# Past keys of the paged cache loaded two rows to a partition in a hybrid decoder step on Trainium2

## The reference

```python
k_past = cache_k_diff[l][page_table].reshape(db, PAST_LEN, N_HEADS_DIFF, 2, HEAD_DIM)
v_past = cache_v_diff[l][page_table].reshape(db, PAST_LEN, N_HEADS_DIFF, DIFF_V_DIM)
...
s_past = jnp.einsum('bqhcd,bkhcd->bchqk', q, k_past, preferred_element_type=jnp.float32) * SCALE
...
p = jax.nn.softmax(jnp.concatenate([s_past, s_new], axis=-1), axis=-1)
w = p[:, 0] - lam * p[:, 1]
o = (jnp.einsum('bhqk,bkhe->bqhe', w[..., :p_len], v_past.astype(jnp.float32))
     + jnp.einsum('bhqk,bkhe->bqhe', w[..., p_len:], v_new.astype(jnp.float32)))
```

## Time and profile before

| | |
|---|---|
| median of 3 runs | 1122.25 us (1115.1, 1124.65, 1122.25) |
| the profiled execution | 1113.92 us, its span 1112.1 us |
| TensorE matmul / VectorE / ScalarE / GpSimd busy | 969.6 / 668.9 / 505.7 / 133.9 us |
| DMA packets | 174933, 310.98 MB, 280 GB/s in the mean |
| key pages from the cache | 256 transfers of 256 KB, the last issued at 439.7 us |
| value pages from the cache | 256 transfers of 256 KB |

### The profile page before, as it was taken

How to read it: one execution, slowest core, us unless ns; L and a number is a source line. 1 busy time by engine, 2 the same in 40 slices (tenths; PEclk the granted TensorE clock), 3 DMA queues, 4 the chain that set the end, 5 groups by cost and what they waited for, 6 DMA issues and landing times.

```text
span 1112.1 us, 29337 instructions
## 1 busy us (share of the span) xinstructions
PE 969.6 (87%) x11050; PEld 858.7 (77%) x11050; DVE 668.9 (60%) x1627; ACT 505.7 (45%) x1116; POOL 133.9 (12%) x69
## 2 busy tenths in 40 slices
PE   3989898998887779887889667899999999999995
PEld 3978787777764557676667554699999999999994
DVE  5389645675458887754346445788888888700003
ACT  5654543374125656645234262455555555611123
POOL 1322111111000010002111000000000000133330
PEclk8999999999988999888899787899999999999997
DMA  8699999999999999888979798386768686974632
GB/s 249 248 314 346 320 328 344 358 340 334 317 340 338 337 365 329 301 273 293 327 245 298 221 255 223 123 302 264 301 263 301 263 301 252 325 248 159 228 128 85
DMA packets 174933, 310.98 MB, mean 280 GB/s; under 512 B 13601, under 2 KB 87714, under 8 KB 173282
## 3 DMA queue, kind: packets, MB, share of 16 engines
q1 hardware_dynamic: 172898, 305.24, 80.3%
q10 hardware_dynamic: 1920, 4.20, 1.4%
HBM read 302.30 MB, written 73.92 MB: 338 GB/s over the span
## 4 chain that ended last, share of the span: by engine, by line
PE 32%; issue 30%; DMA 11%; SPq 11%; DVE 7%; ACT 7%; ACTq 0%; POOL 0%; DVEq 0%; POOLq 0%
PE ps L1383 11%; DMA v_ring<-in_cache_v_diff 6%; SPq L666 5%; PE ps L1038 5%; PE ps L1270 4%; PE ps L1232 4%; SPq L768 4%; DVE kt_sb L2153 2%; ACT q_st L1678 2%; PE ps L1189 2%; DMA k_ring<-in_state_v_win 2%; DMA k_ring<-in_cache_k_diff 2%; PE ps L1115 1%; DMA v_ring<-in_state_v_win 1%; ACT s_sb L1723 1%
## 5 line engine op out<-in xcount | busy, mean ns | idle before, releaser
L2153 DVE STREAM_TRANSPOSE kt_sb<-k_ring 128x512 f32<-128x512 f32 x336 | 220.5, 691 | 86.5 <-DMA k_ring<-in_cache_k_diff 37.4
L1270 PE MATMUL ps<-v_ring,pt_sb 128*32 128x128 f32 (+1 forms) x2496 | 98.8, 306 | 62.1 <-DMA v_ring<-in_cache_v_diff 49.3
L1270 PEld LDWEIGHTS ps<-v_ring,pt_sb 128*32 128x32 f32 (+1 forms) x2496 | 75.7, 121 | 78.1 <-issue 67.8
L1038 PE MATMUL ps<-h_hi,w_hi 128*128 128x288 f32 x384 | 124.4, 324 | 1.9 <-DVE h_lo L2006 1.9
L1038 PE MATMUL ps<-h_lo,w_hi 128*128 128x288 f32 x384 | 115.0, 299 | 0.0
L1038 PE MATMUL ps<-h_hi,w_lo 128*128 128x288 f32 x384 | 114.7, 299 | 0.0
L1232 PE MATMUL ps<-kt_sb,q_st 128*32 128x128 f32 (+1 forms) x2816 | 97.0, 281 | 10.2 <-DVE q_st L2163 4.6
L989 POOL TENSOR_TENSOR c_lo<-c_raw,c_hi 128x1408 fp32r<-128x1408 f32 x14 | 46.6, 3332 | 440.2 <-ACT c_hi L1781 440.2
L1232 PEld LDWEIGHTS ps<-kt_sb,q_st 128*32 128x32 f32 x2816 | 72.9, 114 | 28.2 <-issue 19.9
L1038 PEld LDWEIGHTS ps<-h_hi,w_hi 128*128 128x128 f32 x384 | 74.0, 193 | 16.1 <-issue 13.8
L949 POOL TENSOR_TENSOR w_lo<-w_raw,w_hi 128x1024 fp32r<-128x1024 f32 x24 | 57.3, 2390 | 229.5 <-ACT w_hi L1492 229.5
(11 more groups left out here) (236 smaller groups left out, 2289.4 us busy)
## 6 DMA issues: line engine op xcount, KB each, us to landing
k_ring<-in_cache_k_diff SPq DMA_DIRECT2D x256, 256.0 KB, 5.5
v_ring<-in_cache_v_diff SPq DMA_DIRECT2D x256, 256.0 KB, 5.5
out_k_win_sample<-in_state_k_win SPq DMA_DIRECT2D x32, 1020.0 KB, 8.3
out_v_win_sample<-in_state_v_win SPq DMA_DIRECT2D x32, 1020.0 KB, 8.5
k_ring<-in_state_k_win SPq DMA_DIRECT2D x32, 512.0 KB, 7.7
w_raw<-in_w_in SPq DMA_DIRECT2D x24, 512.0 KB, 6.3
g_raw<-in_w_gate SPq DMA_DIRECT2D x11, 1024.0 KB, 5.2
g_raw<-in_w_up SPq DMA_DIRECT2D x11, 1024.0 KB, 5.2
```

The costliest lines, as they stand in the source:

```text
L1038: last = nc.tensor.matmul(M[c][:, 0:HALF], wt, act[:, k, c * HALF:(c + 1) * HALF], start=k == 0 and at_first, stop=k == KT - 1 and act is ...
L1270: last = nc.tensor.matmul(O[32 * f:32 * f + 32, P * h:P * h + P], pt_sb[0:rows, 4 * f + b, :], values[:, f * P:(f + 1) * P], start=g == 0 ...
L2153: V.transpose(kt_sb[:, i, :], k_ring[:, i, :]).then_inc(kt_done, 1)
```

## The change

The past keys of the cache (`it < 4`) go two rows to a partition: page `i` goes to the 64 even partitions if `i` is even and to the 64 odd ones if it is odd, and its rows `2 u` and `2 u + 1` go to the two slots `i - i % 2` and the next. A slot of `k_ring` then holds every second row of two pages, half each, so a transpose waits for both pages of its pair, and a load waits until both slots of its pair have been turned. The transposes of slots 1 and 2 of a half exchange their places in `kt_sb`. The matmuls of the scores write their 4 x 32 columns with steps, as (slot, u, c) into (u, slot, c), c being two neighbouring columns; the result stands in `S` in the order that the values have, and `keep_scores` reads it straight instead of by steps of 32. The windowed items stay as they were.

```diff
                         src = state_pair(sk, q, i)
-                    at_first = i - (it >= 4 and n == 4)
-                    sp.dma_start(k_ring[:, at_first:i + 1, :].squeeze(1) if at_first == i else k_ring[:, at_first:i + 1, :], src)\
-                        .then_inc(k_landed[i], 16)
+                    if it < 4:
+                        dst, src = k_ring[i % 2:P:2, i - i % 2:i - i % 2 + 2, :], src.rearrange("(u r) c -> u r c", r=2)
+                    else:
+                        dst = k_ring[:, i - 1:i + 1, :] if n == 4 else k_ring[:, i, :]
+                    sp.dma_start(dst, src).then_inc(k_landed[i], 16)
...
-                        sp.wait_ge(kt_done, PAGE_NO[last, i] + 1 if i % 4 < pages_of(last) else half_end(last, h))
+                        sp.wait_ge(kt_done, PAGE_NO[last, i | 1] + 1 if i % 4 < pages_of(last) else half_end(last, h))
...
-                        last = nc.tensor.matmul(S[32 * f:32 * f + 32, c0:c0 + 32 * n], q_st[:, h, f, r, :],
+                        scores = S[32 * f:32 * f + 32, c0:c0 + 32 * n]
+                        if it < 4:
+                            scores = scores.rearrange("p (u x c) -> p x u c", x=4, c=2)
+                        last = nc.tensor.matmul(scores, q_st[:, h, f, r, :],
                                                 kt_sb[:, 4 * h:4 * h + n, c:c + 32], start=r % 2 == 0, stop=r % 2 == 1)
...
-                at_load = key_load(t, i)
-                dve.wait_ge(k_landed[at_load], K_LANDS[t, at_load])
+                for page in (i - i % 2, i | 1) if t < FIRST[4] else (key_load(t, i),):
+                    dve.wait_ge(k_landed[page], K_LANDS[t, page])
                 if t:
                     dve.wait_ge(scored if i >= 4 else half_scored, t)
-                V.transpose(kt_sb[:, i, :], k_ring[:, i, :]).then_inc(kt_done, 1)
+                to = i - i % 4 + (0, 2, 1, 3)[i % 4] if t < FIRST[4] else i
+                V.transpose(kt_sb[:, to, :], k_ring[:, i, :]).then_inc(kt_done, 1)
...
-                    last = V.tensor_tensor_reduce(out=s_sb[:, c:c + 32 * n].rearrange("p (j x) -> p j x", x=n),
-                                                  in0=S[:, 32 * n * k:32 * n * (k + 1)].rearrange("p (x j) -> p j x", x=n),
-                                                  in1=mask.rearrange("p (j x) -> p j x", x=n), scale=1.0, scalar=-3e38,
+                    x = n if it >= 4 else 1
+                    last = V.tensor_tensor_reduce(out=s_sb[:, c:c + 32 * n].rearrange("p (j x) -> p j x", x=x),
+                                                  in0=S[:, 32 * n * k:32 * n * (k + 1)].rearrange("p (x j) -> p j x", x=x),
+                                                  in1=mask.rearrange("p (j x) -> p j x", x=x), scale=1.0, scalar=-3e38,
```

## The result

The kernel with the change takes 1148.05 us (median of 6 runs, 1144.77 to 1155.47) beside 1116.94 us of the kernel before (median of 6, 1111.86 to 1124.65): a ratio of 1.0276, 95% interval 1.0226 to 1.0325, so 31 us slower. The times of a kernel spread by over 1% between runs, so ratios of medians are compared, and a trace is one execution. I had predicted 1120 and no change. The profiled span is 1147.5 us, against 1112.1.

The account below looks back on a forecast made before the run. From 150 to 440 us SP's issuing and the 16 DMA engines were taken to bind in series. -5.6 - 1 + 0 + 3 + 1 + 1 + 0 = -1.6 us on the profiled 1113.92 gave 1112.3, on the median 1120; range 1105 to 1144.

Parts of the forecast that it names:

- the working on SP: 150 to 440 us: SP's issues and reads counted as about 263 of 290 us, leaving about 27 us in hand.
- the price 0 for the 0.14 us more of each key: Past-key issues on SP: 23 us more on 165 keys, taken as hidden inside SP's 27 us in hand.
- issues longer than their median mostly gone: Sign expected in the trace if the forecast held: SP's unusually long issues would mostly disappear.
- The packets: Key transfers in 4 KB instead of 2 KB packets, 414 against 393 GB/s: saves 5.6 us after 150 us, 1 before.
- The issue of a key: SP's key load at L768: from 0.333 to 0.471 us with 64 partitions, priced 0.
- SP becomes the bound: Rival: key issues above 0.50 us, up to 0.602, overfill SP from 150 to 440 us; 1138, chance 0.18.
- rises over 0.5 (slower): Sign that the prediction is wrong: L768's median key issue above 0.5 us, making the kernel slower.
- The pair waits: Waiting for both pages: transposes 3 us after 150 us and 1 before, loads 1 us before and 0 after.
- The stepped scores: Score matmuls writing pairs of columns eight apart: still 1.01 us per 32, cost 0.
- the straight reading: VectorE's four evacuations of a quad (L2190) read in sequence instead of by steps of 32: 0.

Follow-up runs that it names:

- experiment 6: Changed kernel with SP's groups of four values moved so that both keys of a pair are issued back to back: 1.0383 of the kernel before.
- experiment 4: Kernel before with key and value page numbers read in every quad: 1.0210, with both pair waits 1.0291; its table compares SP's instructions and waits across traces.
- experiment 7: Two of eight keys issued by ScalarE in the kernel before (0.9993) and the changed one (1.0382), by GpSimd in the kernel before (0.9941).

## Why the prediction was wrong

**The step that failed** is the end of the working on SP: "The other 27 us are issues that took longer than their median (...), which I read as SP held back because the engines were full. SP thus has about 27 us in hand". From that came the price 0 for the 0.14 us more of each key. Half the bytes left both the time and the long issues about as they were, so the bytes that the engines move weren't their reason, and added work of SP's wasn't taken up by them: 35 more reads between 150 and 440 us (22 us) took only some 5 us out of the long issues, and the kernel was 23 us slower. The longer key issues took more out, 18 us of 39 over all keys, as "issues longer than their median mostly gone" had foreseen; but SP's instructions up to the last key still grew by 27 us, and that was paid. The rows of before could not have told this: SP waits for semaphores for 4 us of 290, which says that SP is busy or held, but not which. The term measures +23 us (1.0210 of 1112; from 18 to 28 by its interval), taken from the repeated reads, which add 27 us to SP up to the last key as the change does.

**The packets** (-5.6 - 1): they came as told and no gain of theirs is seen; half of the key bytes was worth nothing in the kernel before. No run shows whether 4 KB packets would move at 414 GB/s here, as SP asks for less than the 2 KB ones moved.

**The issue of a key** (0.471 us from the 64-row load): 0.485 measured in the median. The median was right and its price wrong. The rival "SP becomes the bound" had the mechanism, but made it depend on an issue over 0.50 us, as did the sign "rises over 0.5 (slower)". The repeated reads leave the key issue at 0.333 and cost 2.1%, so there is no such threshold. The rival gave 1138, 10 us too low.

**The pair waits** (3 + 1 + 1 = 5 us): 13 and 12 us alone, 9 us beside the reads (1.0291 - 1.0210; about 2 to 16 by the two intervals). Probably mis-sized. I priced a transpose later and a load later, each against its own cover; that the two act on each other as a loop, load after transpose after landing of the pair, is argued and not shown. The later landing of pages 2 and 4 in the second stretch is there as VectorE's 59.9 us, and taking it away gave nothing back (experiment 6).

**The stepped scores** (0) and the straight reading (0) were right.

The sum by what was measured: 23 for SP's time, 9 for the pair waits, 0 for packets and scores: 32 us, where the change measures 31. Each term is uncertain by 5 to 7 us, so that they meet within 1 us is luck; the table in experiment 4 is the better support.

**The scale.** I made the sum against one profiled execution and moved it to a median of three runs, 8 us above. With all six runs the kernel before stands at 1117, from where the same sum would have given 1115: the forecast was 28 us too low by its number, and the change was under-priced by 33. That the first three runs stood 5 us higher brought the number nearer by luck.

## What to carry to other kernels

A queue that issues transfers is a server with a load of its own: count its issues with their real pitch (0.52 and 0.79 us here) and with their mean, not only their median. If it hardly waits for a semaphore, suspect it to be full, even if the engines behind it show a share of 1.00. Don't take unexplained long pieces of work for reserve before an experiment has shown them to give way; halving the bytes and adding to the issuer's work by something neutral are two cheap ones. That added work is paid doesn't mean that work taken off is given back: in experiment 7 most of it turned into waits for the next in line. When an added burden shows no effect, look in the trace first whether it ran.

## What the runs showed of the hardware

- The issue of a 256 KB page takes SP 0.333 us in the median with 128 partitions of 2 KB and 0.485 with 64 (every second) of 4 KB; with 64 of 2 KB (128 KB) 0.481, and with 128 of 1 KB 0.333. The time goes by the form in partitions, not by bytes, and fewer packets cost more. The means lie closer, 0.443 and 0.525 us.
- A DMA share of 1.00 at 342 GB/s didn't mean engines that could move no more: with SP relieved it was 359 at a share of 1.02, and with half the key bytes the share was still 0.86 at 270.
- A read of page numbers into SP's registers costs 0.53 us for 8 and 0.97 for 16.
- The score matmuls (fp32, 32 stationary and 128 moving columns) take the same 1.01 us for 32 whether their output in PSUM is plain, in pairs of columns eight apart, or in single columns four apart.
